# Moving the split weights and activations of a two-block transformer kernel to other SBUF byte offsets

## What is computed

```
def first_block(x, c, w_ada, ...):
    mod = silu(c) @ w_ada + b_ada                      # 6 rows of shifts, scales, gates
    h = modulate(rms_norm(x, pre_norm_mix), shift_m, scale_m)
    q, k, v, gates = split(h @ w_in)
    o = concatenate([nsa_mixer(...), moba_mixer(...)]) @ w_o
    x = x + gate_m * rms_norm(o, post_norm_mix)
    h = modulate(rms_norm(x, pre_norm_ffn), shift_f, scale_f)
    f = square(relu(h @ w_up)) @ w_down                # 2048 -> 8192 -> 2048
    return x + gate_f * rms_norm(f, post_norm_ffn)

def second_block(x, ...):
    u = rms_norm(x, norm_mix_pre)
    sb, fox, rw, gates = split(u @ w_in)
    y_a, y_b, y_c = stick_breaking(sb), forgetting_attention(fox), rwkv7_time_mix(rw)
    m = g_a * (y_a @ w_branch_a) + g_b * (y_b @ w_branch_b) + g_c * (y_c @ w_branch_c)
    x = x + rms_norm(m @ w_out, norm_mix_post)
    hdn = square(relu(rms_norm(x, norm_mlp_pre) @ w_mlp_up))
    return x + rms_norm(hdn @ w_mlp_down, norm_mlp_post)
```

## Time and profile before

| | us |
|---|---|
| median of 3 runs | 2974.82 |
| lowest, highest | 2969.61, 2979.16 |
| the profiled execution | 2979.43 |
| its span, first to last instruction | 2977.6 |

### The profile page before, as it was taken

The page is one execution under the profiler, slowest core; times in us unless marked ns, Lnnn a source line. Parts: engine busy times, 40 slices in busy tenths (PEclk is TensorE's granted clock), DMA queues, the critical chain, the costliest instruction groups (busy, mean ns, idle before and its releaser), DMA issues.

```text
span 2977.6 us, 50952 instructions
## 1 busy us (share of the span) xinstructions
PE 2888.0 (97%) x22340; PEld 2662.0 (89%) x22340; DVE 1663.8 (56%) x1484; ACT 1279.9 (43%) x1210; POOL 132.7 (4%) x111
## 2 busy tenths in 40 slices
PE   6899999999999999999999999999999999999998
PEld 5899987899889997889999889999888998899887
DVE  7878987795444454455455654444745444444444
ACT  3334444444434543346354544444344443344433
POOL 0011110000000000000022320000000000000000
PEclk8789999999999999999999999999999999999999
DMA  9999768596556665545451016556554555566553
GB/s 353 384 313 307 265 224 309 178 364 226 189 192 194 190 195 183 195 168 184 152 173 68 10 45 198 191 190 225 170 189 140 194 195 188 196 190 193 184 188 123
DMA packets 300453, 596.74 MB, mean 200 GB/s; under 512 B 12144, under 2 KB 17776, under 8 KB 299760
## 3 DMA queue, kind: packets, MB, share of 16 engines
q1 hardware_dynamic: 294864, 587.83, 58.6%
q10 hardware_dynamic: 5408, 6.23, 0.8%
HBM read 583.80 MB, written 6.29 MB: 198 GB/s over the span
## 4 chain that ended last, share of the span: by engine, by line
PE 84%; DVE 7%; ACT 3%; DMA 3%; issue 2%; POOL 0%; SPq 0%; ACTq 0%; DVEq 0%
PE ps L2276 29%; PE ps L2229 26%; PE ps L2792 9%; PE ps L2376 4%; PE ps L2391 2%; DVE ada_acc L1483 2%; DVE wL L1325 2%; PE ps L2913 2%; ACT wH L765 2%; PE ps L2672 2%; PE ps L2352 1%; DMA ada<-w_ada 1%; DMA raw<-w_up 1%; PE ps L2253 1%; PE ps L2471 1%
## 5 line engine op out<-in xcount | busy, mean ns | idle before, releaser
L1325 DVE TENSOR_TENSOR wL<-raw,wH 128x2048 fp32r<-128x2048 f32 x436 | 1004.2, 2303 | 1120.2 <-ACT wH L765 1115.9
L765 ACT ACTIVATE wH<-raw 128x2048 fp32r<-128x2048 f32 x436 | 837.7, 1921 | 1262.9 <-PE ps L2229 456.5
L2276 PE MATMUL ps<-actH,wH 128*128 128x256 f32 x2816 | 779.6, 277 | 4.0 <-DVE wL L1325 3.9
L2276 PE MATMUL ps<-actL,wH 128*128 128x256 f32 x2816 | 777.9, 276 | 0.0
L2276 PE MATMUL ps<-actH,wL 128*128 128x256 f32 x2816 | 777.8, 276 | 0.0
L2276 PEld LDWEIGHTS ps<-actH,wH 128*128 128x128 f32 x2816 | 529.2, 188 | 6.3 <-DVE wL L1325 3.3
L2276 PEld LDWEIGHTS ps<-actL,wH 128*128 128x128 f32 x2816 | 529.3, 188 | 0.1
L2276 PEld LDWEIGHTS ps<-actH,wL 128*128 128x128 f32 x2816 | 529.1, 188 | 0.0
L2229 PE MATMUL ps<-wH,hidH 128*128 128x512 f32 x1024 | 403.4, 394 | 1.3 <-DVE wL L1325 1.3
L2229 PE MATMUL ps<-wH,hidL 128*128 128x512 f32 x1024 | 400.4, 391 | 0.0
L2229 PE MATMUL ps<-wL,hidH 128*128 128x512 f32 x1024 | 397.4, 388 | 0.0
(11 more groups left out here) (419 smaller groups left out, 3670.0 us busy)
## 6 DMA issues: line engine op xcount, KB each, us to landing
raw<-w_in SPq DMA_DIRECT2D x96, 1024.0 KB, 5.1
ada<-w_ada SPq DMA_DIRECT2D x80, 1024.0 KB, 8.3
raw<-w_up SPq DMA_DIRECT2D x64, 1024.0 KB, 5.3
raw<-w_down SPq DMA_DIRECT2D x64, 1024.0 KB, 5.1
raw<-w_mlp_up SPq DMA_DIRECT2D x64, 1024.0 KB, 5.3
raw<-w_mlp_down SPq DMA_DIRECT2D x64, 1024.0 KB, 5.1
raw<-w_gates SPq DMA_DIRECT2D x48, 1024.0 KB, 5.2
raw<-w_o SPq DMA_DIRECT2D x16, 1024.0 KB, 6.9
```

The lines of the kernel that those rows point to most:

```text
L765: nc.scalar.activation(wH[:, s % SPLIT if L[name]["spg"] > 1 else r % SPLIT, :, :], raw[:, slot, :, :], ACT.Copy).then_inc(wh_ready, 1)
L1325: nc.vector.tensor_tensor(wL[:, b, :, :], raw[:, slot, :, :], wH[:, b, :, :].bitcast(F32), ALU.subtract).then_inc(wl_ready, 1)
L2276: ins = nc.tensor.matmul(out, w[:, b, k, cols], v[:, kk, :], start=(kk == 0 and j == 0 and n % 2 == 0), stop=(kk == STEP_K * spg - 1 and j ...
```

## The change

No instruction is added, removed or moved: each engine has the same rows in the same order. Only byte offsets in the partition change. HIGH_AT and LOW_AT go. A gap of LOW_ACT = 128 bytes comes ahead of `actL`, one of SPLIT_AT - LOW_ACT = 64 ahead of `wH`, none ahead of `wL`. `raw` and `wH` therefore begin 128 bytes further up, `wL` and all behind it stay where they were. `hidH` stays, `hidL` and `o` move 128 bytes down, `yL` 128 up. The rwkv tiles that share the ring's space move 128 up with it, but `uf`, `ST` and `Bc` keep their place.

```diff
-HIGH_AT, LOW_AT = 64, 192
+LOW_ACT, SPLIT_AT = 128, 192
...
     actH = new("actH", [P, KT, T], F32R)
+    top[0] += LOW_ACT
     actL = new("actL", [P, KT, T], F32R)
     RING0 = top[0]
     raw = new("raw", [P, RAW, STEP_K, GC])
-    top[0] += HIGH_AT
+    top[0] += SPLIT_AT - LOW_ACT
     wH = new("wH", [P, SPLIT, STEP_K, GC], F32R)
-    top[0] += LOW_AT - HIGH_AT
     wL = new("wL", [P, SPLIT, STEP_K, GC], F32R)
...
-    hidH = at("hidH", [P, HT, T], F32R, R0 + HIGH_AT + 128)
-    hidL = at("hidL", [P, HT, T], F32R, R0 + 32 * 1024 + LOW_AT + 128)
-    o = at("o", [P, TT, D], F32, R0 + 64 * 1024 + LOW_AT + 128)
+    hidH = at("hidH", [P, HT, T], F32R, R0 + SPLIT_AT)
+    hidL = at("hidL", [P, HT, T], F32R, R0 + 32 * 1024 + SPLIT_AT)
+    o = at("o", [P, TT, D], F32, R0 + 64 * 1024 + SPLIT_AT)
...
-    yL = at("yL", [P, KT, T], F32R, R0 + 68 * K1)
+    yL = at("yL", [P, KT, T], F32R, R0 + 68 * K1 + LOW_ACT)
...
-    rtop[0] += LOW_AT
+    rtop[0] += SPLIT_AT - LOW_ACT
     uf, ST = ring("uf", [P, RHEADS * RHEAD]), ring("ST", [P, RJ, P])
```

More of the change, by code:

```diff
@@ L235, in build_program @@
     sqx = at("sqx", [P, TT, D], F32, R0 + 32 * 1024)
-    sqo = at("sqo", [P, TT, GC], F32, R0 + 80 * 1024 + LOW_AT + 128)
+    sqo = at("sqo", [P, TT, GC], F32, R0 + 80 * 1024 + SPLIT_AT)
     out_f = at("out_f", [P, KT, T], F32, R0)
-    hid = at("hid_sq", [P, GT * T], F32, R0 + 80 * 1024 + LOW_AT + 128)
+    hid = at("hid_sq", [P, GT * T], F32, R0 + 80 * 1024 + SPLIT_AT)
     sq = at("sq", [P, KT, T], F32, R0)
@@ L319, in build_program @@
     Xm, W1 = ring("Xm", [P, MATS, CHUNK]), ring("W1", [P, MATS, CHUNK])
-    lw0, lw = at("lw0", [P, 3, RJ * P], F32, R0 + 76 * K1), ring("lw", [P, 3, RJ * P])
+    lw0, lw = at("lw0", [P, 3, RJ * P], F32, R0 + 76 * K1 + LOW_ACT), ring("lw", [P, 3, RJ * P])
     BT0, KT0 = at("BT0", [P, RJ, T], F32, R0 + 80 * K1), at("KT0", [P, RJ, T], F32, R0 + 82 * K1)
```

## The result

The changed kernel takes 3021.9 us against 2977.0 before, ratio 1.0151 with a 95% interval of 1.0131 to 1.0171. The forecast was 2971, the range ended at 2997: it is 45 us slower, and the prediction was wrong. Each side has four runs, all within 8 us of their median.

The account below looks back on a forecast made before the run. TensorE's own pace was taken to bound the kernel. Terms 0 + 0 + 0 - 3.6 us took the profiled 2979.4 to 2975.8, and the median, 4.6 us lower, to 2971; range 2956 to 2997.

Parts of the forecast that it names:

- What bounds the kernel: Whole kernel: 84% of the chain that ended last is TensorE, with down and up layers as unbroken runs of matmuls.
- 256-column term: Up layers, branches, w_in2 and others, 13,824 matmuls: operands stay 64 apart, so 0; lower end a loss of 11 us.
- The sign that I had named for it: Profile after: the prediction is wrong if the 256-column pace moves at all by a nanosecond.
- Rival four: 256-column layers: such a layer loses its pace, up to 11 us, total 2986; chance 0.05.
- 512-column term: MLP down layers: wH,hidH falls from 393 to 389.5 ns on 1,024 matmuls, 3.6 us gained.
- Rival three: Down layers: moving operand and neighbouring load collide at equal remainders, 9.2 us slower, 2984, range to +22; chance 0.20.
- Rival one: TensorE: operand remainders do nothing, unequal product times come from place in the order; total 2975; chance 0.22.
- `w_out2` and `w_o`: These two layers, 384 matmuls each: operands 64 apart before and after, so 0, within ±4 us.
- VectorE and ScalarE: Reads and writes of the splits: 0, with L1325 at 2,292 and L765 at 1,923 ns after.
- Transfers: Landings of raw moving from remainder 128 to 0, in up_0 and the front: taken as 0.
- rival two: up_0 and front: landing at 0 pays, up to 15.5 us (10 and 5.5), total 2959, or 2967 at half; chance 0.17.

Follow-up runs that it names:

- e3: Kernel before with weights, actH, actL, hidH, hidL all at remainder 128 and yL at 0; 3043.9 us against 2982.2.
- e2: Kernel before with the activations' part alone: actL at 0, hidL at 64, weights kept at 192 and 64; 3065.4 us against 2982.2.
- e4: Kernel before with weights, actH and actL at remainder 64, hidH and hidL at 192; 3066.3 us against 2982.2.
- e10: Kernel before with two overlapping places per wL slot, 128 bytes apart, chosen by layer, hidH and hidL at 192; 2969.0 us against 2975.3, ratio 0.9976.
- e9: e5 with yH and yL at 128 and one 512-column matmul ahead of up_1 and up2_1; 2990.4 us, kernel before 2975.3.
- e11: As e9, but eight one-column matmuls instead of the wide one ahead of up_1 and up2_1; 2984.0 us, kernel before 2982.6.
- e5: Kernel before with wH, wL, hidH, hidL all at 192, actH and actL at 128, yH and yL at 64; 2991.3 us against 2979.7.
- e1: Kernel before with the weights' part alone: wH and wL at 64, activations at 128, hidL at 192, but yL at 0; 3030.6 us against 2982.2.
- e8: Kernel before with weight halves exchanged (wH 64, wL 192), hidH and hidL at 64, yH and yL at 0; 3045.8 us against 2979.7.
- e6: Kernel before with hidH and hidL both at 192, yH and yL both at 0; 2999.1 us against 2979.7.

## Why the prediction was wrong

- **What bounds the kernel** was right: TensorE's own pace, in unbroken pieces. It holds after too, 86% of the chain.
- **The 256-column term is the step that failed.** I took 0, because "only which of the two is ahead changes", and bounded a loss by `w_in2`'s 0.8 ns a matmul, 11 us. It was 3.6 to 4.5 ns a matmul, +44.5 us in the profiled executions. I read load and stream both busy 173.70 of 173.70 us as a sign that nothing disturbs them. It is none: e3's `up_1` goes at 120.0 ns, with the remainders at which the 512-column layers are at their best. The lower end came from spreads inside the kernel before, in which every 256-column layer had one and the same constellation; they could not show what another costs. A price that no row shows had no end in those rows. The sign that I had named for it, a 256-column pace that moves by a nanosecond, is what came.
- **Rival four**, "a 256-column layer loses its pace", had the right place, a chance of 0.05 and a price of 11 us. The price was too low by four times.
- **The 512-column term** had the right sign and half the size. I said 389.5 ns and 3.6 us; it came to 389 ns three times, and 1.7 us on each piece of 768, about 6.5 us over the four down layers. The records give 5 ns less for a triple, the starts 6.5 (3 × 2.2): the ends are modelled, so the sum should have gone by the pace. The reason given, a matmul's own two operands, does not hold: e2 put a second pair apart and kept 228.9 ns. Only "all alike" is borne out, so the right sign was in part luck.
- **Rival three**, equal remainders collide, is wrong for the down layers, where I had put it. In 256-column layers equal remainders are slow (e3, e4: 120.0), but e2, where no two operands of a matmul or of its neighbours are alike, is slower still (120.9), so equality is not the reason there either.
- **Rival one**, remainders do nothing, is refuted by every kernel here. The Trainium skill's rule (page "TensorE: Matmul & The Clock Gate", section "Step-by-step: what each phase is for") is that loading the next weights takes no bandwidth from the running matmul. What I drew from it, that remainders could not matter, is wrong for these fp32r streams: with the same instructions the pace goes from 113.4 to 120.9 ns by addresses. No run shows whether it is the load that takes from the stream.
- **`w_out2` and `w_o`** were put at 0 ± 4 us: 77.91 for 77.42 us in `w_out2`, within.
- **VectorE and ScalarE** at 0: right, 2,292 ns again, and 1,917 for 1,923. Over all thirteen kernels the split in `down_0` lasts 2,292 to 2,294 ns. (The 7 ns between `hidL` and `actL` are six elements' worth at 1.1 to 1.2 ns each, not twenty.)
- **Transfers, rival two**: `up_0` moves 353 GB/s at a share of 1.00 where it moved 361 at 1.02, now paced by TensorE (busy 92.00 of 92.00 us). A gain hidden behind the slower TensorE is not excluded there, since no kernel tried a landing at 0 with the fast pace. In the front, 0 to 150 us, where the share is 1.02 before and after, it is 374 GB/s for 369; e10, with `raw` at 128 as before, has 372. The rival's full price there, 5.5 of 150 us, would be some 383 GB/s, and is not there; a gain of one per cent would not show against such a spread. Its 10 us in `up_0` stay untested.

What stays open is the mechanism itself: which of TensorE's two reads gives way, and why addresses matter. The remainder modulo 256 is the prediction's measure; the tables fit it, but no kernel moved a tile by 256 bytes to test it. The runs show the paces, that they depend on differences between remainders, on the number of moving columns and on how a piece begins. e9 and e11 differ in the kind, the number and the length of what stands ahead of the piece (0.87 us and 1.68 us), and e9's first two loads each come 0.24 us late; which of these picks the pace was not found. e5's `up_0` shows that a wait of 0.1 us can change it.

## What to carry to other kernels

Where matmuls and their weight loads run back to back, the byte offsets of their operands are a parameter worth several per cent of such a stretch (113.4 to 120.9 ns; the whole kernel took 2.8% longer in e2 and e4): measure the pace (an unbroken piece of the chain divided by its matmuls) for each shape of matmul apart, since the best offsets for 512 columns were nearly the worst for 256. A term that no row shows has no bound from rows in which nothing of the kind varies; widen the range there, and multiply by the count before calling it small: 4 ns on 13,824 matmuls is 55 us. Prefer offsets that gave the fast pace in every long piece of every kernel (192, 64 over 128, 128 here) to ones that may give it.

## What I had not expected of the hardware

- The same 1,536 matmuls at the same addresses take 180.91 or 174.20 us, with and without eight one-column matmuls ahead of them (e11, e5).
- A long piece holds its pace: the six sixths of `up_1` go at 117.0 ns each in the changed kernel, at 117.8 in e1, at 118.9 in e8 and at 113.3 to 113.4 in e11, over 1,536 matmuls.
- The rwkv stage had a mean granted clock of 0.94 in one profiled execution and 0.99 in another, 6.5 us apart (197.0 and 190.5), with the same placement of its own tiles but one, `lw0` (e6 and before).
